# Conformer convolution steps of both halves at other places in VectorE's order

## The reference, cut to what matters

```python
z_a, z_b, z_c, z_d = _split(hn @ w_in[i], [A_COLS, B_COLS, C_COLS, D_COLS])
o_a = gmlp_spatial_gating(z_a, ...)
o_b = gated_deltanet(z_b, ...)
o_c = rwkv7_time_mix(z_c, ...)
o_d = conformer_conv(z_d, ...)

def conformer_conv(z, conv_w, conv_b, ln_g, ln_b):
    z1, z2 = jnp.split(z, 2, axis=-1)
    h = z1 * jax.nn.sigmoid(z2)
    h = causal_depthwise_conv(h, conv_w) + conv_b      # 31 taps, 256 channels
    h = layer_norm(h, ln_g, ln_b, LN_EPS)
    return jax.nn.silu(h)
```

## Time and profile before

| | us |
|---|---|
| median of 3 runs | 3497.77 |
| lowest and highest of them | 3496.14, 3498.61 |
| the profiled execution, its own time | 3498.63 |
| its span, first to last instruction | 3496.8 |

### The profile page before, as it was taken

How to read it: one execution, slowest core, us unless ns; L and a number is a source line. 1 busy time by engine, 2 the same in 40 slices (tenths; PEclk the granted TensorE clock), 3 DMA queues, 4 the chain that set the end, 5 groups by cost and what they waited for, 6 DMA issues and landing times.

```text
span 3496.8 us, 27790 instructions
## 1 busy us (share of the span) xinstructions
PE 3339.9 (96%) x10820; PEld 1650.8 (47%) x10820; DVE 1477.5 (42%) x2407; ACT 698.1 (20%) x1155; POOL 746.2 (21%) x623
## 2 busy tenths in 40 slices
PE   8989897899899999999999999999998999999996
PEld 3445463784344444444444555544553444444442
DVE  2375839552543443443326454422125333333313
ACT  3333332521110100101213234212223000000002
POOL 0000000003333423321210000021015524343203
PEclk9999898999999999999999999999998999999998
DMA  3211101052011111121212111222110111111112
GB/s 128 64 44 37 36 28 60 16 171 80 25 42 42 48 37 48 42 70 45 72 60 73 49 49 49 80 78 72 48 48 12 48 48 41 44 48 36 48 60 84
DMA packets 179635, 193.61 MB, mean 55 GB/s; under 512 B 5553, under 2 KB 172977, under 8 KB 178993
## 3 DMA queue, kind: packets, MB, share of 16 engines
q1 hardware_dynamic: 179504, 191.83, 17.1%
HBM read 185.53 MB, written 6.29 MB: 55 GB/s over the span
## 4 chain that ended last, share of the span: by engine, by line
PE 88%; DVE 8%; ACT 2%; POOL 1%; issue 1%; DMA 0%; SPq 0%; DVEq 0%; POOLq 0%
PE psum L1726 21%; PE psum L3261 19%; PE psum L178 12%; PE psum L2221 7%; PE psum L374 6%; PE psum L3288 3%; PE psum L1767 3%; PE psum L388 2%; PE psum L1755 2%; DVE arena L1392 1%; DVE arena L1292 1%; DVE arena L1290 1%; PE psum L526 1%; PE psum L3218 1%; PE psum L3179 1%
## 5 line engine op out<-in xcount | busy, mean ns | idle before, releaser
L1726 PE MATMUL psum<-arena 128*128 128x512 f32 x1736 | 748.3, 594 | 9.1 <-DVE arena L2014 9.0
L3261 PE MATMUL psum<-arena 128*128 128x512 f32 x1568 | 680.5, 597 | 13.4 <-ACT arena L3367 8.7
L1726 PEld LDWEIGHTS psum<-arena 128*128 128x128 f32 x1736 | 330.6, 191 | 426.5 <-issue 423.3
L275 POOL TENSOR_TENSOR arena<-arena 128x512 f32<-128x512 f32 (+1 forms) x310 | 372.8, 1236 | 590.3 <-DMA arena<-mlp_w 251.2
L3261 PEld LDWEIGHTS psum<-arena 128*128 128x128 f32 x1568 | 299.9, 192 | 394.1 <-issue 384.9
L178 PE MATMUL psum<-arena 128*128 128x512 f32 x1024 | 442.6, 592 | 0.0
L1937 DVE TENSOR_TENSOR arena<-arena,psum 128x512 f32<-128x512 f32 x336 | 221.2, 684 | 459.9 <-PE psum L1726 276.7
L3524 DVE TENSOR_TENSOR arena<-arena,psum 128x512 f32<-128x512 f32 x288 | 189.5, 684 | 515.0 <-PE psum L3261 316.1
L374 PE MATMUL psum<-arena 128*128 128x512 f32 x768 | 337.1, 599 | 3.6 <-DVE arena L1146 3.6
L178 PEld LDWEIGHTS psum<-arena 128*128 128x128 f32 x1024 | 194.6, 190 | 241.7 <-issue 241.3
L2221 PE MATMUL psum<-arena 128*128 128x512 f32 x576 | 254.8, 602 | 0.0
(11 more groups left out here) (449 smaller groups left out, 3166.3 us busy)
## 6 DMA issues: line engine op xcount, KB each, us to landing
arena<-w_in SPq DMA_DIRECT2D x42, 1024.0 KB, 5.3
arena<-mlp_w SPq DMA_DIRECT2D x36, 1024.0 KB, 5.2
arena<-w_out SPq DMA_DIRECT2D x16, 1024.0 KB, 5.0
arena<-w_ffn_gate SPq DMA_DIRECT2D x11, 1024.0 KB, 5.3
arena<-w_ffn_up SPq DMA_DIRECT2D x11, 1024.0 KB, 5.3
arena<-w_ffn_down SPq DMA_DIRECT2D x12, 768.0 KB, 4.4
arena<-w_ple_gate SPq DMA_DIRECT2D x8, 1024.0 KB, 5.1
arena<-xa_wq SPq DMA_DIRECT2D x8, 1024.0 KB, 5.0
```

Source lines behind the costliest of these rows:

```text
L275: return g.tensor_tensor(to[:, 0:kn, :], block_of(*a), block_of(*b), op)
L1726: mm = nc.tensor.matmul(ps, left, right, start=(k == 0), stop=(k == kn - 1))
L3261: mm = nc.tensor.matmul(ps, left, right, start=(k == 0), stop=(k == 3))
```

## The change

Only VectorE's list of calls is touched. The steps, their operands and their number stay the same, as do the orders of TensorE, ScalarE, GpSimd and SyncE.

```diff
             sums(0)
             bonus(0)
+            some(taps, 16)
             conv("k", 1)
             dn_final(0)
             decayed(0)
             conv("v", 1)
+            some(taps, 62)
             spread_out(0)
-            some(taps, 62)
             rw_grams(0)
...
             taps = taps_of(1)
-            some(taps, 8)
+            some(taps, 42)
             solve("rw", 0)
             carry("rw", 0)
+            some(taps, 62)
             layer("gm", 1)
...
             mix("rv", 2, 1)
-            some(taps, 16)
             mix("rx", 3, 1)
-            some(taps, 62)
             layer("cf", 1)
```

## The result

| | before | after |
|---|---|---|
| median, us | 3498.19 (4 runs, 3496.14 to 3499.62) | 3461.83 (4 runs, 3458.86 to 3462.91) |
| span of the profiled execution | 3496.8 | 3459.4 |

The ratio is 0.9895 with a 95% interval of 0.9878 to 0.9912: faster by 1.1%, that is by 36.4 us in the medians and 37.4 us in the spans. The forecast was 3467.2, its range 3461 to 3475. The time lies in the range, near its fast end, and the gain is 5.8 us larger than the sum said.

What follows compares the result with a forecast made beforehand. TensorE bounds the kernel (88% of the span), so only its waits for VectorE count: 14.1 - 3.3 - 1.8 + 3.9 + 15.75 + 2.0 = 30.6 us off 3497.8 gives 3467.2 us, range 3461 to 3475.

Steps and rivals of the forecast that it cites:

- First half, 14.1 us: At L490, Grams to next projection take 11.31 us in place of 25.41 without the 24 steps: 14.1 us gained.
- First half, cost 0 of the new places: Sixteen and eight steps fit VectorE's idle time ahead of 301.42 and 338.95, with 2.3 and 4.9 us to spare.
- Second half, the stop at the solve, 3.3 + 1.8 us: Forty steps, slowed by `keys(1)`, make TensorE wait 3.3 us at the solve; a low clock costs 1.8 us more.
- (a): At L601 in the second half, the mix ends earlier without sixteen steps ahead of it: 3.9 us gained.
- (b): At L628 in the second half, the wait for the last convolution step goes: 15.75 us gained.
- (c): L628 itself runs at the 2.4 GHz level without the stop, 3.60 in place of 5.62 us: 2.0 us gained.
- rival 1: Clock stays up at the solve, perhaps also at L601 (up to 2.9 us): 3465.4 or 3462.5 us; chance 0.26.
- Rivals 2 and 4: Larger solve stop, 3469 to 3472 us, chance 0.16; steps slow throughout, 3503 us at 1.7 us each, chance 0.02.
- Rival 3: Only one place pays, another late input replacing L490's or L628's wait: 3481 or 3485 us; chance 0.08.
- Rival 5: The change does not do what it says; given no weight, as VectorE's order shows the steps moved.

Runs made afterwards that it cites:

- e1: Only the first half's part of the change, second half's steps left as before, against the kernel before: 3484.77 us against 3497.38, ratio 0.9963.
- e7: The changed kernel with all 24 first-half steps ahead of conv k and none ahead of spread_out: 3460.74 us, one run.
- e5: The changed kernel with dn_decays(1) moved from ahead of the 42 steps to behind the 24th of them: 3468.88 us, one run.
- e3: The changed kernel with one more VectorE wait, after the 24th of the 42 steps ahead of the solve: 3468.7 us, one run.
- e2: Only the second half's part of the change, first half's steps left as before, against the kernel before: 3474.25 us against 3497.38, ratio 0.9934.
- e4: The changed kernel with 48 in place of 42 steps ahead of the solve and 14 in place of 20 behind the carry: 3463.93 us, one run.
- e6: The changed kernel with 54 in place of 42 steps ahead of the solve: 3471.12 us, one run.
- e8: The changed kernel with key_norm(1) and both cf layer norms also moved earlier: 3450.45 us against 3497.91 for the kernel before, ratio 0.9864.

## Why the prediction was right, and where it was wrong

**First half, 14.1 us: right.** 25.41 - 11.31 = 14.10 us, to the hundredth, from the second half's row. e1 has it alone: 13.9 us in the span, 12.6 us in the medians.

**First half, cost 0 of the new places: right.** 2.50 us and 4.97 us of idle time are left where 2.3 and 4.9 were forecast. e7 shows that it was a cautious reading: the prediction counted only the idle time up to L1164 at 301.42, and the idle time further on counts as well.

**Second half, the stop at the solve, 3.3 + 1.8 us: wrong.** The step that failed carries the first half over to the forty steps: "six steps from 158.22, with `keys(0)` from 158.77 beside them, took 7.35 us in place of 4.0, so 3.3 us are added". Nothing was added: the forty took 26.59 us. The row was right but its situation was another. It shows GpSimd coming up at the start of a chain; here it came up in the middle, and waited 17 us. e5 (the same forty steps, the same phase within a step, but the start of a chain) and e3 (a gap of 0.03 us) both bring the 3.0 us stop and the low clock behind it back. So the size of the term was right and its condition was missing. With it set to 0, the sum is 35.7 us. The prediction had said "I am wrong if [...] the solve's stop is far from 3.3 us": by that sign of its own it was wrong here, whatever the total.

**Second half, (a) 3.9 us: right** (8.22 - 4.34 = 3.88). **(b) 15.75 us: right.** **(c) 2.0 us: right** (5.62 - 3.70 = 1.9).

**What the sum did not have: 1.2 us at L601.** Its matmuls took 5.58 us in place of 6.78. The prediction had this under rival 1, with "up to 2.9 us" (the first half's L601, at 198.74 in the trace of before, takes 3.88 us). Less than half of that came, and in no run here more than 1.5 us. The clock was still 1.00 over the 4.3 us ahead of L601 and low only from about 565.8 to 569 us. How long L601 takes is not fixed: 5.34 us in e2, 6.79 us in e3, behind the same wait of 4.34 us. Windows of the changed kernel:

```profile
561.50:565.80 4.30, 0.01 (x1) 0.00 (x0) 0.88 (x2) 3.23 (x4) 0.00 (x0) 1.00 0.64 197
565.80:567.00 1.20, 1.15 (x2) 0.66 (x3) 0.00 (x0) 0.00 (x0) 0.00 (x0) 0.53 1.08 383
```

14.1 + 3.9 + 15.75 + 1.9 + 1.2 = 36.85 us, and L419 of `key_norm(1)` starts at 582.94 in place of 619.76, 36.82 us earlier. Everything behind moved with it; the last 0.6 us of the span's 37.4 are scattered.

**The total, and luck.** That the time lies in the range is in part luck. 5.1 of the 5.8 us that the sum missed belong to a stop that did not come, and neither the forecast nor a rival had a case without any stop. The range reached down to 3461 because rival 1 counted a stop without a low clock (1.8 us) and 2.9 us at L601; what came was no stop at all (5.1 us) and 1.2 us at L601.

**The rivals.** Rival 1 came closest (3462.5 to 3465.4 for 3461.8), though for one of its two places for another reason: the clock did not fall at the solve because there was no stop. Rivals 2 and 4 rested on VectorE being slowed by GpSimd more than the forecast had it, the opposite of what happened. e3 and e5 show what the forecast itself describes, a stop of 3.0 us with the low clock behind it: 3468.7 and 3468.9 us, one run each, where it gave 3468.0 for the profiled execution. Rival 3, a new wait in place of L490's or L628's, did not come: neither waits. Rival 5 falls with the timeline.

**The page of the Trainium skill.** "SBUF — State Buffer", section "Who interferes with whom", says that the two engines' shared port pair is an exclusive lock: the one that issues first has it for its whole instruction, and the other blocks. For single instructions the runs agree: in e5 a step that takes 0.75 us alone took 2.39 us, when it came up 0.12 us behind a product of 1.97 us. But by that sentence, as I read it, GpSimd would get its turn after one step. Here it waited for 26 steps, 17 us. The page also says that the order of issue decides who blocks; the prediction read the rule only for what it would cost VectorE.

## What to carry to other kernels

Price moved work by the same work elsewhere in the trace, but check that the situation is the same, too: here a row gave 14.10 us exactly and another gave 3.3 us that did not come, because it showed the start of a chain and not its middle. In these runs one unbroken chain of VectorE instructions with two SBUF inputs kept out a GpSimd product that came up in its middle; one semaphore wait within the chain let it in and cost TensorE a stop of 3.0 us and 1.8 us of low clock behind it. The chain spares VectorE at GpSimd's cost, so before making one look for who waits for GpSimd. And where a range holds, check which terms made it hold: here one term of 5.1 us was wrong and the total hid it.

## What the runs showed of the hardware

- A GpSimd product of two SBUF operands that comes up in the middle of a gapless chain of VectorE steps with two SBUF inputs is held until the chain's end: recorded lengths 19.18, 19.17, 19.90, 27.13, 19.17 and 19.18 us for 1.90 us of work (changed kernel, e2, e4, e6, e7, e8). No step of these chains was slowed (0.76 us at most). It ran beside L1319, whose second input is in PSUM.
- It gets in at a gap of 0.03 us (e3), and behind the first step of a chain (e5, and `keys(0)` in every trace here). After it is in once, its second product gets in as well, 2.23 us long, between two steps without a visible gap; each costs VectorE about 1.6 us. Why the first steps of a chain are open and later ones are not was not settled.
- TensorE's stop of 2.97 us ended with the clock still at 1.00, and it was at 0.51 for the 2.6 us behind it (e5); a stop of 2.98 us at L442 did the same in e4 (1.00, then 0.50). Within the 7.63 us of e6 it fell to a mean of 0.69. The stops of 4.34 us ahead of L601 were followed by 5.34 to 6.79 us for the same twelve matmuls. For a sum to within 2 us this can't be foretold from the length of a stop.
